# Expert layer of a two-block model: 2 MB weight tiles in five slots, gather and sum in pieces between the passes

## The reference, cut to what matters

```python
def swiglu(t, w_gu, w_down):
    a, g = jnp.split(t @ w_gu, 2, axis=-1)
    return (jax.nn.silu(a) * g) @ w_down

def moe_swiglu(h, w_router, w_gu, w_down):
    t = h.reshape(b * s, d)                               # 256 x 1024
    logits = (t @ w_router).astype(jnp.float32)
    top_logit, top_idx = lax.top_k(logits, TOP_K)         # 2 of 8
    top_w = jax.nn.softmax(top_logit, axis=-1)
    gate = jnp.einsum('tk,tke->te', top_w, jax.nn.one_hot(top_idx, N_EXPERTS, ...))
    out = jnp.zeros_like(t)
    for e in range(N_EXPERTS):
        out = out + gate[:, e:e + 1] * swiglu(t, w_gu[e], w_down[e])
    return out
```

## Time and profile before

| | us |
|---|---|
| three runs | 2047.01 (median), 2045.9, 2048.48 |
| profiled execution, device time | 2047.62 |
| its span, first to last instruction | 2045.8 |
| TensorE busy | 1983.7 (97%), granted clock 0.994 of full speed |
| VectorE / ScalarE / GpSimd busy | 836.6 / 324.9 / 65.6 |
| expert layer's passes, first to last | 928.75 to 1599.1 |
| DMA | 485.66 MB, mean 237 GB/s |

### The profile page before, as it was taken

How to read it: one execution, slowest core, us unless ns; L and a number is a source line. 1 busy time by engine, 2 the same in 40 slices (tenths; PEclk the granted TensorE clock), 3 DMA queues, 4 the chain that set the end, 5 groups by cost and what they waited for, 6 DMA issues and landing times.

```text
span 2045.8 us, 31213 instructions
## 1 busy us (share of the span) xinstructions
PE 1983.7 (97%) x13540; PEld 1253.2 (61%) x13540; DVE 836.6 (41%) x1514; ACT 324.9 (16%) x718; POOL 65.6 (3%) x72
## 2 busy tenths in 40 slices
PE   9999999999999999999999989999988999999998
PEld 4888786998458877863333333333333544855997
DVE  4555645456635466561010001110000499444446
ACT  2242111111103411210000000000000232420100
POOL 0000000000000000000000000000000035000000
PEclk9999999999999999998999999999999999999999
DMA  7533543444335244109999999899999732226240
GB/s 311 212 111 137 226 165 139 165 175 161 118 134 196 104 193 198 42 25 419 421 420 420 420 421 396 353 420 420 420 421 421 322 123 108 108 92 248 103 186 21
DMA packets 57036, 485.66 MB, mean 237 GB/s; under 512 B 6544, under 2 KB 6704, under 8 KB 9280
## 3 DMA queue, kind: packets, MB, share of 16 engines
q1 hardware_dynamic: 53424, 464.67, 56.3%
q0 software_dynamic: 3472, 18.95, 2.3%
HBM read 482.54 MB, written 1.05 MB: 236 GB/s over the span
## 4 chain that ended last, share of the span: by engine, by line
PE 87%; DMA 10%; DVE 1%; issue 1%; ACT 1%; SPq 0%; DVEq 0%; ACTq 0%
PE bank L392 46%; PE pair L392 41%; DMA weights<-in_moe_down 8%; DMA weights<-in_moe_up 2%; ACT hT L2945 0%; SPq L3475 0%; DMA const<-in_const 0%; DVE att L1869 0%; DVE h L2260 0%; DVE h L1750 0%; DVE probT L1686 0%; DVE h L1742 0%; DVE att L1870 0%; DVE big L2603 0%; ACT att L3236 0%
## 5 line engine op out<-in xcount | busy, mean ns | idle before, releaser
L392 PE MATMUL bank<-weights,att 128*32 128x512 f32 (+2 forms) x4228 | 392.6, 525 | 15.4 <-issue 13.9
L392 PEld LDWEIGHTS bank<-weights,att 128*32 128x32 f32 (+1 forms) x4228 | 145.6, 110 | 244.2 <-issue 215.3
L392 PE MATMUL pair<-weights,big 128*32 128x512 f32 (+2 forms) x1606 | 232.9, 587 | 24.2 <-DMA weights<-in_moe_down 24.2
L392 PEld LDWEIGHTS pair<-weights,big 128*32 128x32 f32 (+1 forms) x1606 | 90.3, 120 | 153.4 <-issue 149.9
L392 PE MATMUL bank<-hT,weights 128*128 128x128 f32 (+1 forms) x976 | 164.9, 325 | 0.0
L392 PEld LDWEIGHTS bank<-hT,weights 128*128 128x128 f32 x976 | 144.8, 191 | 17.2 <-issue 6.6
L2244 DVE TENSOR_TENSOR big<-head_gain,bank 128x256 f32<-128x256 f32 (+1 forms) x66 | 24.9, 377 | 295.4 <-ACT head_gain L3194 295.4
L392 PE MATMUL pair<-weights,hT 128*128 128x512 f32 (+2 forms) x336 | 137.9, 568 | 1.5 <-ACT hT L2945 1.2
L3194 ACT ACTIVATE head_gain<-bank 128x256 f32<-128x256 f32 (+1 forms) x66 | 23.0, 349 | 550.6 <-PE bank L392 550.6
L392 PEld LDWEIGHTS pair<-weights,hT 128*128 128x128 f32 x336 | 63.3, 190 | 71.5 <-issue 70.0
L392 PE MATMUL pair<-hT,weights 128*128 128x128 f32 (+1 forms) x784 | 105.0, 293 | 0.9 <-ACT hT L2945 0.8
(11 more groups left out here) (478 smaller groups left out, 2422.7 us busy)
## 6 DMA issues: line engine op xcount, KB each, us to landing
weights<-in_moe_up SPq DMA_DIRECT2D x176, 1024.0 KB, 16.7
weights<-in_moe_down SPq DMA_DIRECT2D x88, 1024.0 KB, 18.5
weights<-in_w_in SPq DMA_DIRECT2D x17, 2048.0 KB, 7.5
weights<-in_ffn_up SPq DMA_DIRECT2D x11, 2048.0 KB, 7.3
weights<-in_even_in SPq DMA_DIRECT2D x10, 2048.0 KB, 13.4
weights<-in_mem_wkv SPq DMA_DIRECT2D x8, 2048.0 KB, 7.3
weights<-in_odd_in SPq DMA_DIRECT2D x8, 2048.0 KB, 7.2
norm_par<-in_norms POOLq DMA_DIRECT2D x11, 1024.0 KB, 7.6
```

The costliest lines, as they stand in the source:

```text
L392: ins = pe.matmul(o, lhsT, rhs, **flags)
```

## The change

1. Expert tiles are whole slots. Each up chunk has four loads of 2 MB. The down side has five steps of four k-rows (2 MB a tile) and a last one of two (1 MB a tile). The slots that the layer uses follow on from those before it (`few_slot`), five in all instead of ten halves. The loads fall from 264 to 136.
2. SyncE reads a rank just before it first needs it; the first load stands behind one rank instead of eight.
3. A second `few_T` and a second `put_T` exist, in buffers that are idle then. The eight gather pieces of group 1 stand in group 0's chunks 1 to 8, between pass 1 and pass 2; its put matrices in chunk 10. The four sum pieces of group 0 stand in group 1's chunks 1, 3, 5 and 7, at the same place. Group 0's put matrices are made after the first pass and not before it.
4. Pass 1's block of the put matrix is made twice, each with zeros in the other half, so that all sum products have 128 rows. That is eight transposes in a group and not six, four more memsets on VectorE in a group, and a copy of 1024 columns instead of 768.
5. VectorE copies the gathered pieces of group 0 before it makes the gated matrices.

The core of the diff (the other lines rename, or move the same code):

```diff
-SLOTS, PUT_SLOTS = 2 * P + 2 * QUAD, 3 * P
+SLOTS, PUT_BLOCKS = 2 * P + 2 * QUAD, 4
-FEW_STEPS_UP, FEW_STEPS_DOWN = 2 * HID_CHUNKS, KF // 2
-FEW_TILES = N_GROUPS * GROUP * (FEW_STEPS_UP + FEW_STEPS_DOWN)
+FEW_STEPS = HID_CHUNKS + len(FEW_DOWN)
+FEW_TILES = N_GROUPS * GROUP * FEW_STEPS
+FEW_FIRST = NSLOT - FEW_TILES % NSLOT
+PUT_CHUNK = HID_CHUNKS - 1
+SUM_CHUNKS = (1, 3, 5, 7)
...
+            def few_pass(q, steps, slots, name=None):
+                for last, j, ins in steps:
+                    if last and (q, j) in ((1, 2), (2, 1)):
+                        ins.then_inc(sems(f"few{slots[q - q % 2]}_used"), 1)
+                if name:
+                    end_late(ins, name)
+                if q and name:
+                    slot_owed[0] = f"few{slots[q - q % 2 + 1]}_used"
+                elif q:
+                    ins.then_inc(sems(f"few{slots[q - q % 2 + 1]}_used"), 1)
+
+            def few_up(g, c):
+                slots = [few_tile(), few_tile()]
+                for q in range(PASSES):
+                    if q == 2:
+                        slots += [few_tile(), few_tile()]
+                    name = ("few_up", g, c, q)
+                    o = begin(banks, name, late=True)
+                    few_pass(q, few_up_pass(g, c, q, o, slots), slots, name)
+                    if q == 0 and c:
+                        few_hidden_T(g, c - 1)
+                    if q == 0 and (g, c) == (0, 0):
+                        few_put(0)
+                    if q == 1 and g == 0 and 1 <= c <= KD:
+                        few_gather(1, c - 1)
+                    if q == 1 and (g, c) == (0, PUT_CHUNK):
+                        few_put(1)
+                    if q == 1 and g == 1 and c in SUM_CHUNKS:
+                        few_sum(0, *divmod(SUM_CHUNKS.index(c), 2))
...
                     few_group(0)
-                    few_gather(1)
-                    few_sum(0)
                     few_group(1)
-                    few_sum(1)
+                    for t in range(NT):
+                        for i in range(2):
+                            few_sum(1, t, i)
...
                     for copy_of in range(2):
-                        o = gated[g][:, t, 2 * P + 64 * copy_of:2 * P + 64 * copy_of + 64].rearrange("p (y n) -> p y n", y=2)
+                        own = 2 * P + (P + LIGHT) * copy_of
+                        other = 2 * P + LIGHT + LIGHT * copy_of
+                        o = gated[g][:, t, own:own + LIGHT].rearrange("p (y n) -> p y n", y=2)
+                        ve.memset(gated[g][:, t, other:other + LIGHT], 0.0)
...
+                            if x not in mine:
+                                mine[x] = sp.value_load(order_i[0:1, r:r + 1], min_val=0, max_val=N_EXPERTS - 1)
+                            src = d[name][bass.ds(mine[x], 1)].rearrange("e p n -> p (e n)")[:, at:at + width]
+                            s = few_slot(first, i)
+                            if taken[s]:
+                                sp.wait_ge(*L.at(f"few{s}_used", taken[s]))
+                            else:
+                                sp.wait_ge(*L.at(f"slot{s}_used", sum(j % NSLOT == s for j in range(first))))
+                            sp.dma_start(weights[:, s, 0:width], src).then_inc(sems(f"few{s}_landed"), 16)
```

More of the change, by code:

```diff
@@ L92, with few_slot, few_uses @@
 C_END = 1256
-def half_uses(m):
-    return len(range(m, FEW_TILES, NHALF))
+def few_slot(first, i):
+    return (first + FEW_FIRST + i) % NSLOT
+def few_uses(first, s):
+    return sum(few_slot(first, i) == s for i in range(FEW_TILES))
 def weight_tiles(k_tiles, widths, group):
@@ L1210, in few_up_pass @@
                             flow = tile.rearrange("p (a h n) -> p a h n", a=2, h=2)[:, :, j // 2, :]
[L1211 to L1215, removed]
+                        ins = mm(out, few_T[g][k][:, quad_columns(q, j)], flow, start=(k == 0), stop=(k == KD - 1))
@@ L1229, in few_group @@
-            def few_group(g):
[L1230 to L1235, removed]
-                for c in range(HID_CHUNKS):
[L1237 to L1260, removed]
@@ new lines, in few_down_pass @@
+                                     weights[:, slots[owner(q, j)], at:at + 512],
+                                     start=(k0 + k == 0), stop=(k0 + k == KF - 1))
+                            yield k == nk - 1 and i == (0 if q == 1 else 1), j, ins
+            def few_pass(q, steps, slots, name=None):
[8 more added lines that the diff above has]
+                    ins.then_inc(sems(f"few{slots[q - q % 2 + 1]}_used"), 1)
@@ L1268, in few_group @@
                             pe.wait_ge(*emptied(("few_hidT", g, HID_CHUNKS - 1, i)))
-                    halves = [half_tile(), half_tile()]
+                    slots = [few_tile(), few_tile()]
                     for q in range(PASSES):
                         if q == 2:
[L1272 to L1282, removed]
+                            slots += [few_tile(), few_tile()]
+                        few_pass(q, few_down_pass(q, k0, nk, outs[q], slots), slots, ("few_down", g, q) if final else None)
@@ L1283, in few_group @@
                     if n == 0:
                         few_hidden_T(g, HID_CHUNKS - 1)
[L1286 to L1298, removed]
+                    k0 += nk
@@ new lines, in few_sum @@
+            def few_sum(g, t, i):
+                if (t, i) == (0, 0):
+                    pe.wait_ge(*emptied(("few_put", g)))
+                o = begin(banks, ("few_sum", g, i, t), late=True)
+                for q in range(PASSES):
+                    if (t, i) == (0, 0):
+                        pe.wait_ge(*emptied(("few_down", g, q)))
+                    block = (0, 2 + i, 1)[q]
+                    y = few_y[q][:, 0:512] if q == 1 else few_y[q][:, 512 * i:512 * i + 512]
+                    ins = mm(o[:, :], put_T[g][:, block, t * P:(t + 1) * P], y, start=(q == 0), stop=(q == PASSES - 1))
+                end_late(ins, ("few_sum", g, i, t))
@@ L1349, in moe @@
                     L.seen = seen
-                    for m in range(NHALF):
-                        pe.sem_inc(sems(f"half{m}_used"), half_uses(m))
+                    for s in range(NSLOT):
+                        pe.sem_inc(sems(f"few{s}_used"), few_uses(tiles_used[0], s))
                     pe.sem_inc(sems("banks_filled"), IN_FEW["banks_filled"])
```

181 lines of the change are left out of this document (94 added, 87 removed).

## The result

The changed kernel takes 2070.48 us (median of 4 runs, 2068.57 to 2072.51) against 2047.74 for the kernel before: ratio 1.0112, interval 1.0096 to 1.0128. It is slower; the forecast was 2037.0. The profiled execution has a span of 2068.7 against 2045.8: +22.9.

What follows compares the result with a forecast made beforehand. The 16 DMA engines, at 420 GB/s, were taken to bound the expert layer, TensorE second. Terms -9.3 - 8.1 + 2 + 2.5 + 3 - 0.8 = -10.7 us took 2047.62 to 2036.9, given as 2037, range 2027 to 2050.

Steps and rivals of the forecast that it cites:

- Five slots: Slot reuse in up chunks: 19.1 us fits under 19.6, no cost; +2.5 at the seam, +3 at group 1's end.
- rival A: Queue runs dry in every up chunk at pass 1's slot release if landing exceeds 7.8 us: +18, 2055 us; chance 0.14.
- 2 MB loads: Expert weight stream: 2 MB lands in 4.90 us against 4.976 for two of 1 MB, -9.3 us.
- Standstill: Between the two groups: the DMA engines' stop goes as gather and sum move into the chunks, -8.1 us.
- Sum pieces: Group 1's chunks 1, 3, 5, 7: sum pieces between passes lengthen four chunk pairs, 1.2 to 4 us, taken as +2.
- Start: Before the first expert load: reading one rank instead of eight starts loads 3.9 us earlier but is worth 0.
- 128-row products: Group 1's sums: four pieces 0.37 us shorter, partly hidden by VectorE's row work, -0.8 us (0 to -1.5).
- TensorE's clock: Down steps: one longer wait may lower the clock, but slot freeing still fits 19.6; 0, upper bound 10 us.
- Rival B: Expert stream: the bigger loads are not quicker, only -1.4 us in all, 2046 us; chance 0.17.
- C: Seam, group end and sums: no new delays, as loads in flight cover them; -17 us, 2030 us; chance 0.16.
- D: Up chunks: gather pieces wait for VectorE or a bank and stop TensorE; +6, 2043 us; chance 0.06.

Runs made afterwards that it cites:

- e1: The changed kernel with ten places of 1 MB instead of five slots of 2 MB, all else of the change kept: 2034.88 us, ratio 0.9942.
- e5: The changed kernel, still five 2 MB slots, with the first two experts' weights of a group in halves, two to a slot: 2037.03 us, ratio 0.9947.
- e9: e5 with both expert pairs in halves in the down steps and five of eight gather pieces moved there: 2036.9 us, ratio 0.9953.
- e7: e1 with group 1's gather and group 0's sum put back between the groups: 2041.62 us, ratio 0.9967.
- e2: The changed kernel with group 1's gather and group 0's sum put back between the groups, 2 MB tiles kept: 2073.4 us, ratio 1.013.
- e11: The kernel before with one edit, the ranks read as they are needed instead of all eight ahead: 2044.65 us, ratio 0.9983.
- e4: e1 with eight places of 1 MB instead of ten: 2038.23 us, ratio 0.9957.

## Why the prediction was wrong, step by step

**Five slots, "it costs nothing while a load lands in 7.3": this is the step that failed.** The loop was found and set up rightly (rival A, chance 0.14): one slot, released by the second pass, 19.1 against 19.6. It was filled with two numbers that were each too small. Start to issue was 12.0 and not 11.8. The landing was 7.3 from the earlier trace rows, the median of eleven loads alone. Their spread already stood in the trace of the kernel before (view of the loads' line from 280 to 440, all eleven):

```profile
DMA to landing us min/median/max: 7.1/7.3/8.4
```

In the loop it is 7.3 to 10.0 (8.5 in the mean of nine chunks of group 0): the slot is only full when the last of 16 engines is done, and the load ahead lands 2.5 to 4.0 us after the issue. 12.0 + 8.5 + 0.1 to the pass = 20.6, and the chunks of group 0 measure 20.76; where the load came in time, TensorE's own 19.88 set the chunk. A slack of 0.5 us was read as a cover. Its cost in all is the difference of the changed kernel and e1: 35.6 us. In the two profiles the first sum of group 1 starts 36.0 us apart. Of these, 8.7 arise between the starts of chunks 1 and 10 of group 0, 10.6 from there to chunk 1 of group 1 (down steps and seam), 16.5 between chunks 1 and 10 of group 1, and what is ahead and behind differs by less than 0.5 each. So rival A, with +18 for the up chunks, had the place right and the size too small (25.2). The seam shows a wait of 5.93 and then a pass at low clock:

```profile
1267.20 3.64 PE L401 MATMUL pair<-weights,big 128*32 128x512 f32 x32 [1.29 <-DMA weights<-in_moe_down]
1276.77 6.73 PE L401 MATMUL bank<-weights,big 128*32 128x512 f32 x48 [5.93 <-issue]
```

I also argued against rival A that the last engine's work is in the queue already. In a full queue that may be so; this one is nearly drained when the load is issued, and even its first engine is done only 6.7 to 7.4 us later, as in a load alone (6.6 to 6.7).

**2 MB loads, -9.3: the pace was right, the gain was not there.** The first five loads of the changed kernel, queued together, land 4.89 us apart (forecast 4.90), and e5 and e9 move up to 425 GB/s in a window of the up chunks with part of the bytes in whole tiles. But a gather piece costs 1.41 us in place (19.88 against 18.47), not 1.09, which was the pace of eight in a row. So TensorE's own chunk is 19.88, not 19.56, and 19.92 in group 1. Loads of 19.6 gain nothing there. e9 leaves only three pieces in these chunks, which then stand 19.57 apart (transposes at 954.63 and 1111.15), so the pace does show once it may; the time still didn't fall, and that part stays open. The two limits lie within 0.1 us of each other in e1 (eight 1 MB loads: 19.9).

**Standstill, -8.1:** 6.7 by e7 against e1 (5.1 by the ratios). Right, a little large. In the changed kernel itself the seam is 8.3 shorter than in e2, but the pieces save nothing clear of the noise, as group 1's chunks give it back.

**Sum pieces, +2:** in e1 they cost nothing that can be seen, since chunks of 21.38 and 18.47 average 19.92 against 19.90 for the loads. In the changed kernel, against e2, chunks 1 to 10 of group 1 are 11.3 longer with them than without, and the forecast was 2: waits of 3.02, 2.88, 1.33 and 3.25 us follow the four pieces, each one chunk later. Timeline of group 1, the chunk after one with a sum piece:

```profile
1325.84 1.21 PE L401 MATMUL pair<-const,big 128*128 128x128 f32 x6
...
1340.53 7.05 PE L401 MATMUL bank<-weights,big 128*32 128x512 f32 x48 [3.02 <-issue]
1347.37 1.93 PE L401 MATMUL bank<-weights,att 128*32 128x512 f32 x16
1349.23 1.21 PE L401 MATMUL pair<-const,big 128*128 128x128 f32 x6
```

After 3.02 of waiting 48 products take 7.05, at 1.2 GHz for 3.4 us, where they take 5.33 without it: 23.39 for a chunk that is 18.47 by itself.

**Start, 0:** right for the changed kernel: chunk 1 starts at 951.78 (958.78 - 7.0) against 952.04. Its first two tiles are twice as large, and TensorE waits for them until 928.88. Wrong for 1 MB tiles, where e11 shows 2.8.

**128-row products, -0.8:** right. A piece takes 2.57 (above, 1626.29 to the next; the first 2.68) against 2.97. From the first sum to the next stage's first product e1 needs 13.97, the kernel before 14.77 (1613.89 - 1599.12):

```profile
1587.62 1.13 PE L396 MATMUL bank<-prob,gate_tokens 128*128 128x512 f32 x2
...
1601.59 2.25 PE L396 MATMUL bank<-const 128*128 128x128 f32 x18 [3.41 <-DVE h L2284]
```

```profile
1613.89 4.18 PE L392 MATMUL bank<-const 128*128 128x128 f32 x18 [2.63 <-DVE h L2260]
```

**TensorE's clock, 0:** the records of the granted clock have nine stretches of 3.4 us at 1.2 GHz in the layer of the changed kernel, after its first passes, against one in the kernel before, each behind a wait for a load, eight of them of 2.2 us or more:

```profile
1180.69 8.70 PE L401 MATMUL pair<-weights,big 128*32 128x512 f32 x64 [2.59 <-DMA weights<-in_moe_down]
```

Here a pass of 7.07 took 8.70. They follow from the waits and don't start the loss: e5 has four of 3.4 us and one of 6.8 there and stays at 2037. In the changed kernel, where the loop is tight, they can add 1.7 each, 15 at most by this estimate (forecast 0, bound 10). How much of the 35.6 that is was not measured by itself.

Rival B is out by the landings 4.89 apart, C by e1 (the delays are real). D is out as well: in e1 the pieces stay and the time falls, and in the changed kernel no wait of TensorE between 950 and 1620 is put down to VectorE.

## What to carry to other kernels

For a ring of slots, write down for each slot the time from its release to the first product that needs its next tile; here the least of them against the landing time of the slowest engine decided, and not the bytes in flight. A margin of half a microsecond on a landing that repeats twenty times is no margin: take the late landings, not the median. When a transfer is made quicker, look at the second limit first: pieces of work put into its idle time may already have used it up. The fastest version by the medians is e1: the change without the larger tiles, 2034.9 and 2035.9 us in two sets of runs; e5 and e9 come within 2 us of it.

## What the runs showed of the hardware

- Eight MB in places of 1 MB keep the stream at 420 or 421 GB/s in e4's windows from 950 to 1550, but for two after the seam (413 and 417), at 3.3 us over ten MB.
- The 2 MB loads for the tight slot, issued when only the load before is still landing, land after 7.3 to 10.0 us on the last engine (mean 8.5 of 20 in the up chunks), while the first engine is done after 6.7 to 7.4; a small transfer of instructions on single engines falls into some of them (the page's queue q8, 110 packets of 16 KB in the span). That these are a cause was argued from the times of the packets and not tested. The Trainium skill (DMA: Bandwidth & Descriptors, Why a DMA increments its semaphore by 16 and not by 1) says that the landing is complete with the last engine's share; the trace agrees: the load issued at 1045.25 is done on its first engine at 1052.26 and on its last at 1055.23, and the pass starts at 1055.32.
- A wait's length alone does not say whether the clock falls: 3.4 us at 1.2 GHz followed waits of 2.59 and 3.02 us, and one of 1.58; the waits of 1.98 at 1053.35 and of 2.48 at 1240.42 stayed at 2.4 GHz.
